# Prompt attention one query tile of two heads at a time, with the two heads' products issued in turn

## The reference, cut to what matters

```python
def attention_prompt(q, k, v):
    parts = [dilated_branch_prompt(q, k, v, d, w // d) for (w, d) in ATT_BRANCHES]
    out = combine_branches(parts).astype(q.dtype)
...
def combine_branches(parts):
    """Mix dilation branches weighted by their softmax denominators."""
    m = jnp.stack([p_[0] for p_ in parts])
    l = jnp.stack([p_[1] for p_ in parts])
    acc = jnp.stack([p_[2] for p_ in parts])
    w = jnp.exp(m - jnp.max(m, axis=0, keepdims=True))
    den = jnp.sum(w * l, axis=0)
    num = jnp.sum(w[..., None] * acc, axis=0)
    return num / den[..., None]
```

## Time and profile before

| | |
|---|---|
| median of three executions | 3622.04 us |
| the profiled execution, which is its span | 3634.0 us |
| prompt attention in it, first product to last scaling | 364.93 to 594.90, 229.97 us |
| TensorE busy in that stage | 225.05 us |
| VectorE busy in that stage | 102.98 us |
| ScalarE busy in that stage | 92.61 us |
| mean granted TensorE clock in that stage | 0.88 of 2.4 GHz |

### The profile page before, as it was taken

The page is one execution under the profiler, slowest core; times in us unless marked ns, Lnnn a source line. Parts: engine busy times, 40 slices in busy tenths (PEclk is TensorE's granted clock), DMA queues, the critical chain, the costliest instruction groups (busy, mean ns, idle before and its releaser), DMA issues. The chain is left out here.

```text
span 3634.0 us, 54589 instructions
## 1 busy us (share of the span) xinstructions
PE 3381.6 (93%) x20435; PEld 2046.0 (56%) x20435; DVE 2581.0 (71%) x5334; ACT 1309.6 (36%) x2581; POOL 1028.2 (28%) x1074
## 2 busy tenths in 40 slices
PE   7999998869899988799999999997899999999997
PEld 4668664246546654465655555554455555555554
DVE  4222443145442369999999999996888888888887
ACT  3000343132120012367767677663222222222222
POOL 0000000000000000488999989993111111111110
PEclk9999889977799999999999999999999999999998
DMA  3220933542342235478887788879877887788874
GB/s 140 93 98 24 344 120 147 194 163 93 108 161 74 74 125 190 147 249 279 285 291 263 275 279 283 289 257 377 345 289 285 298 299 294 285 298 297 295 283 155
DMA packets 213104, 803.41 MB, mean 221 GB/s; under 512 B 33824, under 2 KB 92320, under 8 KB 169088
## 3 DMA queue, kind: packets, MB, share of 16 engines
q1 hardware_dynamic: 176000, 531.81, 40.5%
q0 software_dynamic: 36864, 268.45, 21.0%
HBM read 665.19 MB, written 201.98 MB: 239 GB/s over the span
## 5 line engine op out<-in xcount | busy, mean ns | idle before, releaser
L1670 PE MATMUL psum<-arena 128*128 128x400 f16 x6144 | 1095.8, 336 | 53.8 <-DVE arena L1718 53.4
L2027 PE MATMUL psum<-arena 128*128 128x400 f16 x6144 | 1049.6, 332 | 27.9 <-DVE arena L2073 27.9
L1670 PEld LDWEIGHTS psum<-arena 128*128 128x128 f16 x6144 | 597.0, 99 | 481.0 <-DVE arena L1718 62.6
L2027 PEld LDWEIGHTS psum<-arena 128*128 128x128 f16 x6144 | 596.5, 97 | 481.0 <-DVE arena L2073 28.3
L1642 POOL TENSOR_SCALAR arena<-arena 128x128 f16<-128x128 f16 x800 | 712.2, 904 | 54.1 <-DVEq L1848 26.3
L116 POOL DMA_INDIRECT arena<-in_experts,arena x256 | 304.1, 1188 | 1176.1 <-DVE arena L149 1079.3
L135 ACT ACTIVATE arena<-arena 128x1 f32<-128x1 f32 x256 | 51.6, 202 | 932.8 <-DVE arena L128 932.7
L149 DVE SCALAR_TENSOR_TENSOR arena<-arena 128x1024 f32<-128x1024 f32 x256 | 331.8, 1296 | 18.6 <-issue 2.8
L2080 DVE TENSOR_TENSOR arena<-arena,psum 128x800 f32<-128x800 f32 x256 | 252.0, 984 | 108.2 <-PE psum L2027 108.2
L128 DVE CUSTOM_DVE_ANT_0 arena<-arena 128x1024 f32<-128x1024 f32 x256 | 311.3, 1219 | 16.2 <-DMA arena<-in_experts,arena 15.3
L1899 ACT ACTIVATE arena<-arena 128x128 f16<-128x128 f16 x800 | 245.1, 388 | 88.9 <-DVE arena L1856 88.7
(11 more groups left out here) (230 smaller groups left out, 3741.1 us busy)
## 6 DMA issues: line engine op xcount, KB each, us to landing
arena<-in_u_feat SPq DMA_DIRECT2D x128, 512.0 KB, 6.7
arena<-in_experts SPq DMA_DIRECT2D x128, 512.0 KB, 5.3
scratch_acts<-arena SPq DMA_DIRECT2D x128, 400.0 KB, 4.1
arena<-scratch_gates SPq DMA_DIRECT2D x32, 1600.0 KB, 7.7
arena<-scratch_acts SPq DMA_DIRECT2D x128, 400.0 KB, 6.7
scratch_gates<-arena SPq DMA_DIRECT2D x48, 1024.0 KB, 6.8
out_k_win_sample<-in_cache_k SPq DMA_DIRECT2D x32, 1022.0 KB, 21.7
out_v_win_sample<-in_cache_v SPq DMA_DIRECT2D x32, 1022.0 KB, 21.2
```

Of the source, the lines that this page charges most:

```text
L1670: last = pe.matmul(psum[:, 2 * p + k, 0:SLD], w[:, s, q, :], xs[:, q, k * SLD:(k + 1) * SLD], start=q == 0 and w is u_hi and xs is x_hi, s ...
L2027: last = pe.matmul(psum[:, 2 * (n % BANKS) + i, 0:SLD], w[:, s, k, q * P:(q + 1) * P], hs[:, s, k, i * SLD:(i + 1) * SLD], start=k == 0 an ...
```

## The change

A step is now a tile `t`: one query tile of both heads of a pair, 32 steps in one loop instead of 64 blocks in two turns. `probs`, `turned`, `shares` and the small vectors have four places instead of two. The scores of the two heads are issued alternately, piece of 512 columns by piece, head 0 into banks 0 and 1, head 1 into banks 2 and 3; the scores of the next tile wait until both heads' scores of the tile before are read. The values products of the two heads are issued alternately, key tile by key tile, and the two products with `ones` follow. The orders of the engines are changed with it. The amount of work per head and tile is the same: the same products, passes and copies in the same shapes.

```diff
-        probs = at(word, 2, SEQ); word += 2 * SEQ
-        turned = at(word, 2, SEQ); word += 2 * SEQ
+        probs = at(word, 4, SEQ); word += 4 * SEQ
+        turned = at(word, 4, SEQ); word += 4 * SEQ
         feat_q, feat_k = m["feat"][:, FQ], m["feat"][:, FK]
-        shares = at(word, 2, P); word += 2 * P
+        shares = at(word, 4, P); word += 4 * P
         spread = at(word, 2, P); word += 2 * P
-        top = at(word, 2, 1); word += 2
-        neg_top = at(word, 2, 1); word += 2
-        total = at(word, 2, 2); word += 4
-        inv = at(word, 2, 2); word += 4
+        top = at(word, 4, 1); word += 4
+        neg_top = at(word, 4, 1); word += 4
+        total = at(word, 4, 1); word += 4
+        inv = at(word, 4, 1); word += 4
...
-        PAIRS = 2
-        BLOCKS = PAIRS * 2 * TT
-        TILES = PAIRS * TT
-        tile = [n // 2 % TT for n in range(BLOCKS)]
-        pieces = [1 if i < 4 else 2 for i in tile]
-        before = [sum(pieces[:n]) for n in range(BLOCKS + 1)]
-        PIECES = before[-1]
-        SPARE = 4
+        TILES = H // 2 * TT
+        width = [(t % TT + 1) * P for t in range(TILES)]
+        pieces = [-(-w // 512) for w in width]
+        before = [2 * sum(pieces[:t]) for t in range(TILES + 1)]
+        buf = lambda t, half: 2 * (t % 2) + half
...
-                scores(0)
-                for n in range(BLOCKS):
-                    if n + 1 < BLOCKS:
-                        scores(n + 1)
-                    turn(n)
-                    if n >= 1:
-                        values(n - 1)
-                values(BLOCKS - 1)
+            def scores(t):
+                pair, i = divmod(t, TT)
+                if t >= 1:
+                    pe.wait_ge(scores_read, 2 * t)
+                for s in range(0, width[t], 512):
+                    e = min(width[t], s + 512)
+                    for half in range(2):
+                        r = slice(64 * half, 64 * half + 64)
+                        last = pe.matmul(psum[:, 2 * half + s // 512, 0:e - s], feat_q[r, pair, i * P:(i + 1) * P],
+                                         feat_k[r, pair, s:e], start=True, stop=True)
+                        if e == width[t]:
+                            last.then_inc(scores_ready, 1)
+
+            def turn(t, half):
+                i = t % TT
+                pe.wait_ge(exp_ready, 2 * t + half + 1)
+                for b in range(pieces[t]):
+                    n = before[t] + half * pieces[t] + b
+                    if n >= 2:
+                        pe.wait_ge(piece_copied, n - 1)
+                    for k in range(4 * b, min(i + 1, 4 * b + 4)):
+                        last = pe.transpose(psum[:, 4 + n % 2, (k % 4) * P:(k % 4 + 1) * P],
+                                            probs[:, buf(t, half), k * P:(k + 1) * P], m["ident"])
+                    last.then_inc(piece_ready, 1)
+
+            def values(t):
+                pair, i = divmod(t, TT)
+                pe.wait_ge(piece_copied, before[t + 1])
+                if t >= 2:
+                    pe.wait_ge(out_copied, t - 1)
+                for k in range(i + 1):
+                    for half in range(2):
+                        pe.matmul(psum[64 * half:64 * half + 64, 6 + t % 2, 0:P],
+                                  at(V0 + k * 512 + pair * P + 64 * half, 64),
+                                  turned[:, buf(t, half), k * P:(k + 1) * P], start=k == 0, stop=k == i)
+                for half in range(2):
+                    pe.wait_ge(share_ready, 2 * t + half + 1)
+                    pe.matmul(psum[64 * half:64 * half + 64, 6 + t % 2, P:2 * P], m["ones"][:, 0:64],
+                              shares[:, buf(t, half), :], start=True, stop=True).then_inc(values_ready, 1)
+
+            scores(0)
+            for t in range(TILES):
+                if t + 1 < TILES:
+                    scores(t + 1)
+                turn(t, 0)
+                if t >= 1:
+                    values(t - 1)
+                turn(t, 1)
+            values(TILES - 1)
...
+            def add_bias(t, half):
+                dve.wait_ge(scores_ready, 2 * t + half + 1)
+                if t >= 2:
+                    dve.wait_ge(piece_ready, before[t - 1])
+                b = buf(t, half)
+                scores = psum[:, 2 * half:2 * half + 2, :].rearrange("p a b -> p (a b)")
+                dve.tensor_tensor_reduce(probs[:, b, 0:width[t]], scores[:, 0:width[t]],
+                                         bias[:, SEQ - width[t]:SEQ], 1.0, LOWEST, ALU.add, ALU.max,
+                                         top[:, b, :]).then_inc(scores_read, 1)
+                dve.drain()
+                dve.tensor_scalar(neg_top[:, b, :], top[:, b, :], -1.0, None, ALU.mult).then_inc(max_ready, 1)
+
+            def share(t, half):
+
+                b = buf(t, half)
+                dve.wait_ge(exp_ready, 2 * t + half + 1)
+                if t >= 2:
+                    dve.wait_ge(values_ready, 2 * (t - 1))
+                dve.reciprocal(inv[:, b, :], total[:, b, :])
+                dve.drain()
+                dve.tensor_scalar(shares[:, b, :], m["ident"], inv[:, b, :], None, ALU.mult).then_inc(share_ready, 1)
+
+            def scale_out(t):
+                pair, i = divmod(t, TT)
+                dve.wait_ge(values_ready, 2 * t + 2)
+                dve.tensor_copy(spread[:, t % 2, :], psum[:, 6 + t % 2, P:2 * P])
+                dve.drain()
+                dve.tensor_tensor(at(XT0 + i * P + pair * T, P), psum[:, 6 + t % 2, 0:P],
+                                  spread[:, t % 2, :], ALU.mult).then_inc(out_copied, 1)
+
+            for t in range(TILES):
+                add_bias(t, 0)
+                add_bias(t, 1)
+                if t >= 1:
+                    share(t - 1, 0)
+                    share(t - 1, 1)
+                if t >= 2:
+                    scale_out(t - 2)
+            share(TILES - 1, 0)
+            share(TILES - 1, 1)
+            scale_out(TILES - 2)
+            scale_out(TILES - 1)
...
+            def exps(t, half):
+                b = buf(t, half)
+                act.wait_ge(max_ready, 2 * t + half + 1)
+                act.activation(probs[:, b, 0:width[t]], probs[:, b, 0:width[t]], ACT.Exp, bias=neg_top[:, b, :],
+                               accum_out=total[:, b, :]).then_inc(exp_ready, 1)
+
+            def copy_pieces(t, half):
+                if t >= 2:
+                    act.wait_ge(values_ready, 2 * (t - 1))
+                for b in range(pieces[t]):
+                    n = before[t] + half * pieces[t] + b
+                    s, e = 512 * b, min(width[t], 512 * b + 512)
+                    act.wait_ge(piece_ready, n + 1)
+                    act.copy(turned[:, buf(t, half), s:e], psum[:, 4 + n % 2, 0:e - s]).then_inc(piece_copied, 1)
+
+            for t in range(TILES):
+                for half in range(2):
+                    if t >= 1:
+                        copy_pieces(t - 1, half)
+                    exps(t, half)
+            copy_pieces(TILES - 1, 0)
+            copy_pieces(TILES - 1, 1)
```

More of the change, by code:

```diff
@@ L505, in _ @@
+            scores(0)
[7 more added lines that the diff above has]
+            values(TILES - 1)
         @block.vector
         def _(dve):
-            dve.sem_inc(scores_read, 2)
             dve.wait_ge(bias_loaded, 16)
[L510 to L548, removed]
@@ L550, in _ @@
+            for t in range(TILES):
[10 more added lines that the diff above has]
+            scale_out(TILES - 1)
         @block.scalar
         def _(act):
-            act.sem_inc(piece_copied, SPARE)
-            act.sem_inc(out_copied, 2)
@@ L555, in _ @@
[L555 to L577, removed]
```

## The result

The kernel after takes 3537.8 us (median of four, 3535.43 to 3545.06) against 3623.68 us (3618.03 to 3638.07) for the kernel before in the same comparison: a ratio of 0.9751, interval 0.9726 to 0.9777. The forecast was 3546 us, so it was 8 us too high, and the direction and the size were right.

What follows compares the result with a forecast made beforehand. TensorE was taken to bound the stage; 134.6 us at full clock, plus 3 for the short count and 16 for low clock, gave 154 us, 76 less than 230, so 3622 - 76 = 3546 us; range 3526 to 3585.

Steps and rivals of the forecast that it cites:

- Products in different groups of the array run at once: TensorE: full overlap, two heads' scores for the time of one, two heads' values for the time of one.
- The rule on weight loads: TensorE values: by the rule the two heads' values, sharing rows, would stay in sequence; the prediction held that the trace disagrees.
- Rival 2: TensorE: scores overlap, values don't; loops sum to 165.5 us, + 35 us, 3581 us; chance 0.07.
- TensorE's loops and VectorE's: Per tile, the larger of both engines' loops: 32.7 us a pair, 130.9 for four; TensorE alone 30.2 us a pair.
- ScalarE and the scores' single set of banks at nothing: ScalarE's 4.5 us in a 4.7 us loop, and scores waiting for both bias passes, were costed at nothing.
- The ends: Stage's start and end: 11.3 us drain from the last scores replaces the last two loops (9.1); the start costs 1.5.
- The clock: Stage: 40 us at half clock, each costing 0.41 us, so + 16 us; bounds 0 and the whole stage.
- The sum: Stage: 134.6 + 3 + 16 = 154 us, 76 less than 230; median forecast 3622 - 76 = 3546.
- Rival 1: Half clock over nearly all of the stage: some 228 us, no change, 3620 us; chance 0.08.
- 3: TensorE: each change of group empties the array at 0.09 us, nothing overlaps; stage about 249 us, 3641 us; chance 0.03.
- rival 2's last sentence: TensorE: if nothing overlaps, loops 190.8 us, + 60, 3606 us; the change only saves shape changes; chance 0.03.
- rival 4: Something unseen in the order of waits, 10 to 30 us; chance 0.07.

Runs made afterwards that it cites:

- experiment 1: Kernel after, with all values products of head 0 issued before those of head 1: 3557.07 us, ratio to before 0.9806.
- experiment 4: Kernel before, with all four pairs in one turn (PAIRS = 4 instead of 2): 3621.12 us, ratio 0.9984.
- experiment 3: Kernel after, with both scores and values products of head 0 issued before those of head 1: 3558.11 us.
- experiment 5: Kernel after, with TensorE issuing scores, transposes and values of head 0, then those of head 1; buffers and other engines' orders kept: 3621.21 us, ratio 0.9986.
- experiment 7: Kernel after, with VectorE making each head's diagonal share matrix twice: 3548.90 us.
- experiment 8: Kernel after, with the last pair's query tiles taken from widest to narrowest: 3532.49 us; repeated 3539.76 us, beside 3537.56 us for the kernel after.
- experiments 1 to 4: First four follow-up kernels, run beside the kernel before at 3630.93 us; the second, kernel after with scores head by head, took 3537.29 us.

## Why the prediction was right, step by step

- **Products in different groups of the array run at once.** Right for both kinds, read from the earlier trace rows beforehand. Two heads' scores take 1.92 us where one head's took 1.91, and values 0.055 us a record.
- **The rule on weight loads.** The Trainium skill, TensorE: Matmul & The Clock Gate, section "Part 3: Packing small matmuls", says that weight loads run beside products in flight only where the row group differs. Rival 2 (3581 us) had the values in sequence by that rule. The kernel after disagrees: 32 values records with 32 weight loads in shared rows take 1.80 us. The same section of the Trainium skill says that products keep the order of the program; the rows of experiment 1 disagree with that too.
- **What the order of issue does.** The prediction took from the meeting places that "there each meeting overlaps only by the few records that the engine sees ahead". That is right, but the number wasn't drawn into the sum of parts: for scores of at most four records a head, and for values of narrow tiles, the lookahead is all that is needed. Standing side by side gives some 60 us (211.5 us of stage in experiment 4 to 151.4 in experiment 3, the two shape changes saved a tile and 7 us less of low clock among them), issuing in turn 19.5 us more. What was expected of experiment 5 speaks of "some five records ahead"; the single records show three still to come, and 0.6 us hidden a tile.
- **TensorE's loops and VectorE's.** I had 32.7 us a pair at full clock; measured are 31.2 (the steps between bias passes of the second and third full pair sum to 31.6 and 31.2). The step that failed is where VectorE waits for the values. The prediction puts the wait ahead of the shares, so that shares and scaling (1.6 us) follow the values. But `share(t)` waits for `values_ready` of 2(t - 1), which the values of tile t-2 fulfil; only `scale_out` waits for those of tile t-1, and only its 0.66 us follow them, as the rows above show. This was to make VectorE the bound in the loops of tiles 0 and 7, with 4.12 and 4.67 us; measured are 3.48 and 4.27, each with a wait for scores at its end, so TensorE sets them (its count was 3.45 and 4.54). Tiles 1 to 6 were 3.13, 3.40, 3.67, 4.30, 4.95, 4.47 and measured 3.01, 3.27, 3.54, 4.34, 4.99, 4.35. So TensorE is the bound in half of the loops, and VectorE has some room (experiment 7) where the text had nearly none.
- **ScalarE and the scores' single set of banks at nothing.** Nearly right. ScalarE's waits for transposes are idle time; TensorE waits 3.0 us for the scores' banks in all, and 1.3 us in the drain for ScalarE's copies.
- **The ends.** 11.3 us behind the last scores; measured 485.7 (end of the last scores) to 497.4, 11.7.
- **The clock.** This was the term most wrong: 40 us at half clock were taken, for 16 us; there were 9.7, which at the 0.44 us of experiment 4 are 4, and perhaps less here, since the 3.4 us in experiment 8 go with 0.8 us. The 0.41 us of the prediction rest on 221 us, which double the products but, against what the text says, not the changes of shape; with them it is 241 us and 0.46, and the measured 0.44 lies between. The joints between pairs, where TensorE has less to do, brought the low clock in none of the profiles with overlap; only the start of the stage did, for 6.8 to 10.2 us in all nine profiles with overlap, and for 17.1 to 34.1 us in the three without.
- **The sum.** The stage was to be 154 us and is 132: 12 too much for the clock, 3 for a count that wasn't short (experiment 4 has 50.5 us a pair where 50.2 were counted), some 6 for VectorE's misplaced wait. This error of 22 us in the stage became one of 8 in the time because of another step: the 76 us were taken off the median, though the profiled execution of before, from which they were counted, lay 12 us over it, and had 54.6 us of low clock. Experiment 4's kernel, without the second low stretch, gains 18.5 us of stage in the profile but only 10 in the median; so a part of what the profile promised was never in the median. The two errors went against each other, so the mechanism was right, but that the forecast came within 8 us is luck.
- **The rivals.** Rival 1 (half clock throughout) and 3 (each change of group empties the array) are out by the rows above. What rival 2's last sentence says of no overlap, 3606 us, experiment 5 bears out in kind: 3621, 15 us more than that and within 0.1% of the kernel before beside it. Some 10 of the 15 are the changes of shape, which that sentence had as saved and experiment 5 doesn't save. Of rival 4, something unseen in the waits, the profile shows nothing: the stage was shorter than its sum.

What stays open: why the low stretch at the start is shorter in the kernels with overlap. No run here separates it from their other differences.

## What to carry to other kernels

Products that use half of the array (64 rows or 64 columns) are worth placing next to a partner that uses the other half: here the pair took the time of one, and neighbours that share a shape also save the change between shapes. With up to four records each, side by side was enough; longer runs had to be issued in turn. After such a halving, look at once at the other engines' orders, since here VectorE came to set half of the loops, with some 13 to 16 us of room left over the stage, and the products left between two groups of transposes were the cover for the copies.

## What the runs showed of the hardware that was not expected

- TensorE starts products out of program order across column groups: in experiment 1, head 0's ones-product at 443.93 us runs ahead of three values records of head 1 that stand before it, and head 1's first values record starts with three of head 0's still to come.
- 36 values and ones records of two heads, to the start of the next kind: 4.06 us by count in sequence, 3.48 us issued head by head, 2.12 us in turn.
- The low clock at the start of this stage lasts anywhere from 6.8 to 34.1 us, and a us of it costs 0.44 us without overlap. In the before kernel's executions beside experiments 1 to 4 the mean clock over the span goes with the time, from 0.958 at 3616 us to 0.951 at 3641: 0.007 of the span is some 50 us more at half clock, by the 0.44 us 22 of the 25 us. So this kernel differs from one execution to the next by more than a small edit of it would show.
